# Expert tiles requested two at a time in a decoder step on one Trainium2 core

## What is computed

```python
q = (xt @ w_query)                         # 8 heads, 256 wide
s1, s2 = q[..., :128] @ k1.T, q[..., 128:] @ k2.T
v1, i1 = top_k(s1, 16); v2, i2 = top_k(s2, 16)
top, pos = top_k(v1[:, None] + v2[None, :], 16)    # 16 experts per head
g = softmax(top)
hid = u_tab[eidx] . xt                     # first layer: one dot product per expert
a = g * gelu(hid)
out = sum(a * v_tab[eidx])                 # second layer
```

## Time and profile before

| | |
|---|---|
| median of 3 runs | 1867.72 us (1864.65 to 1868.74) |
| profiled execution | 1864.95 us, span of the profile 1863.4 us |
| mean granted TensorE clock | 0.960 of full speed |
| TensorE busy | 1691.0 us, 91% of the span |
| VectorE busy | 1397.9 us, 75% |
| ScalarE busy | 776.9 us, 42% |
| GpSimd busy | 570.6 us, 31% |
| moved by DMA | 470.82 MB, mean 253 GB/s |
| requests of expert tiles | 128 of 512 KB, median 6.7 us from issue to landing |

### The profile page before, as it was taken

One profiled execution on the slowest core, in us unless ns is written; L12 is line 12 of the kernel. 1 busy time (PEld: TensorE's weight loads), 2 busy tenths in 40 slices (PEclk: granted clock), 3 DMA queues, 4 the chain that ended last, 5 costly groups with the idle time before them and its releaser, 6 DMA issues. The chain is left out here.

```text
span 1863.4 us, 30406 instructions
## 1 busy us (share of the span) xinstructions
PE 1691.0 (91%) x9914; PEld 1486.2 (80%) x9914; DVE 1397.9 (75%) x3179; ACT 776.9 (42%) x1195; POOL 570.6 (31%) x508
## 2 busy tenths in 40 slices
PE   5997898779799999779989999996899999999994
PEld 4997643449699999779989999996688888888883
DVE  3234267534389999968979888987898999999995
ACT  3222034221444433256657666663333333333333
POOL 0010280000354544433323333332433333333330
PEclk9998899899799999989999999998899999999997
DMA  3242361261343432379998998999999999999992
GB/s 112 97 174 94 121 214 46 83 232 43 116 143 111 138 115 82 124 259 350 345 376 304 366 354 332 380 338 361 363 386 387 384 384 384 384 384 389 385 385 81
DMA packets 195215, 470.82 MB, mean 253 GB/s; under 512 B 17922, under 2 KB 100482, under 8 KB 192558
## 3 DMA queue, kind: packets, MB, share of 16 engines
q1 hardware_dynamic: 124014, 240.30, 36.7%
q0 software_dynamic: 50944, 178.96, 26.0%
q10 hardware_dynamic: 20160, 50.34, 6.9%
HBM read 411.97 MB, written 61.32 MB: 254 GB/s over the span
## 5 line engine op out<-in xcount | busy, mean ns | idle before, releaser
L226 PE MATMUL hp<-mid_hi,uhi 128*128 128x384 f32 x1024 | 355.3, 347 | 12.0 <-issue 6.0
L227 PE MATMUL hp<-mid_lo,uhi 128*128 128x384 f32 x1024 | 345.7, 338 | 0.0
L228 PE MATMUL hp<-mid_hi,ulo 128*128 128x384 f32 x1024 | 344.4, 336 | 0.0
L226 PE MATMUL va<-vhi,ahi 128*128 128x512 f32 x768 | 299.6, 390 | 22.6 <-DVE alo L2010 22.6
L227 PE MATMUL va<-vlo,ahi 128*128 128x512 f32 x768 | 299.4, 390 | 0.0
L228 PE MATMUL va<-vhi,alo 128*128 128x512 f32 x768 | 299.2, 390 | 0.0
L2026 POOL DMA_INDIRECT gathered<-in_v_experts,idx_row x160 | 186.5, 1166 | 323.9 <-DVEq L1981 289.7
L1719 POOL DMA_INDIRECT gathered<-in_u_rows,idx_row x160 | 169.2, 1058 | 312.9 <-DVE hrow L1772 228.0
L226 PEld LDWEIGHTS hp<-mid_hi,uhi 128*128 128x128 f32 x1024 | 193.8, 189 | 17.3 <-DVE ulo L1785 8.6
L1316 ACT ACTIVATE uhi<-uw 128x1024 fp32r<-128x1024 f32 x128 | 135.7, 1060 | 151.9 <-PE hp L228 101.9
L1955 ACT ACTIVATE vhi<-vw 128x1024 fp32r<-128x1024 f32 x128 | 134.8, 1053 | 144.3 <-DMA vw<-in_v_experts 144.1
(11 more groups left out here) (328 smaller groups left out, 3306.2 us busy)
## 6 DMA issues: line engine op xcount, KB each, us to landing
uw<-in_u_experts SPq DMA_DIRECT2D x128, 512.0 KB, 6.7
vw<-in_v_experts SPq DMA_DIRECT2D x128, 512.0 KB, 10.6
hidden_values<-gelu_out ACTq DMA_DIRECT2D x128, 192.0 KB, 5.4
gate_matrix<-gst ACTq DMA_DIRECT2D x12, 2048.0 KB, 12.7
mid_hi<-hidden_values SPq DMA_DIRECT2D x32, 768.0 KB, 11.9
mid_lo<-gate_matrix SPq DMA_DIRECT2D x32, 768.0 KB, 16.6
pw<-in_w_qk SPq DMA_DIRECT2D x16, 512.0 KB, 3.5
qw<-in_w_query SPq DMA_DIRECT2D x16, 512.0 KB, 5.0
```

The costliest lines, as they stand in the source:

```text
L226: nc.tensor.matmul(out, a_hi, b_hi, start=first, stop=False)
L227: nc.tensor.matmul(out, a_hi, b_lo, start=False, stop=False)
L228: return nc.tensor.matmul(out, a_lo, b_hi, start=False, stop=last)
```

## The change

A request now covers two tiles, m and m+1, m even, and fills two neighbouring buffers, r and r+1, with 1 MB. It waits for the low half of tile m-3 (before: the request of m waited for that of m-4, the one of m+1 for that of m-3). Both tiles of a pair count on one semaphore, `u_load[r // 2]`, so ScalarE's high half of either tile waits until the whole pair has landed. The rows read stay 4 KB: the pattern is partition, tile, row.

```diff
-        u_load = [sem(f"u_load{i}") for i in range(UR)]
+        u_load = [sem(f"u_load{i}") for i in range(UR // 2)]
...
         def u_fetch(sp, m, r):
-            sp.wait_ge(u_lo, m + 3 - UR)
-            sp.dma_start(uw[:, r], A["u_experts"][m]).then_inc(u_load[r], 16)
+            sp.wait_ge(u_lo, m + 4 - UR)
+            sp.dma_start(uw[:, r:r + 2], A["u_experts"][bass.ds(m, 2)].rearrange("n p k c -> p n k c")).then_inc(u_load[r // 2], 16)
 
         def u_split_hi(act, m, i, r):
-            act.wait_ge(u_load[r], (m - r) * (16 // UR) + 16)
+            act.wait_ge(u_load[r // 2], (m - r) * (16 // UR) + 16)
...
-                for r in range(UR):
-                    sp.dma_start(uw[:, r], A["u_experts"][r]).then_inc(u_load[r], 16)
+                for r in range(0, UR, 2):
+                    sp.dma_start(uw[:, r:r + 2], A["u_experts"][r:r + 2].rearrange("n p k c -> p n k c")).then_inc(u_load[r // 2], 16)
...
-                    for r in range(RT):
+                    for r in range(0, RT, 2):
                         u_fetch(sp, RT * j + UR + r, r % UR)
-                for e in range(QX + UR):
+                for e in range(0, QX + UR, 2):
                     u_fetch(sp, RT * NH + e, e % UR)
...
-                    for i in range(GTI):
+                    for i in range(0, GTI, 2):
                         u_fetch(sp, G0 + GTI * j + i + UR, slot(half, i))
```

## The result

The changed kernel took 1881.45 us in the median of 20 executions (1871.25 to 1887.29), the kernel before 1866.89 in as many (1864.65 to 1873.72). The ratio is 1.0068, with an interval of 1.0053 to 1.0082: slower by 0.68%, or 12.7 us. (It is taken over all executions; the two medians by themselves are 14.6 us apart.) That lies above the range given, whose upper end was 1875. The profiled execution took 1885.38 us, and its span, 1883.8, is 20.4 longer than the one before.

A forecast was written before the change was run, and what follows sets the result against it. TensorE was taken to bound the gate stage, with the DMA engines close to full, and VectorE the retrieval stage's end. Four terms of 0 left the median at 1867.7 us, range 1862 to 1875.

The forecast's parts named there:

- Part 1: SyncE's requests: 128 become 64 and its issues of about 0.33 us halve, worth nothing by itself; cost 0.
- Parts 1 and 2: The second: at the first request, ScalarE's first high half waits for both tiles, about 1.3 us, covered by GpSimd; cost 0.
- Part 3: Even tiles, requested one tile later, still land in time; second 512 KB adds 1.7 us, under the 3.6 spare; cost 0.
- Rival C: Expert requests served by two of sixteen engines: 24 us per 1 MB, 500 us in all, near 2370; chance 0.01.
- rival A2: Gate stage: even tiles come too late for ScalarE's high half, 8.4 to 20.7 us slower, 1882; chance 0.05.
- Rival B: DMA queues in the gate stage: fewer requests relieve them, TensorE wins back 5.2 us, 1862.5; chance 0.13.
- part 4: Other transfers beside gate stores: help or hurt by at most 7.5 us, gain at most 5.2; taken as 0.
- Rival A: ScalarE's hidden-value stores behind gate stores held up to 1.5 us longer, five times, plus 1.1 for clock: 1876.3; chance 0.13.

The follow-up runs named there:

- the changed kernel's second profile: The changed kernel run again without further edits, against the kernel before on the same chip: 1873.63 us, ratio 1.0043; the profiled execution took 1865.83 us.
- joint landing alone: The kernel before, single requests at their old times, but one semaphore per pair so both high halves wait for both tiles: 1866.58 us, ratio 1.0000.
- one pair alone: The kernel before with one 1 MB request per turn, at i = 8, all others single at old times: 1883.30 us, ratio 1.0089.
- bunched singles: The kernel before with every even tile requested one tile later, still 128 requests of 512 KB; three runs: ratios 1.0009, 1.0018, 1.0008.
- the two runs made for it: Changed kernel with i = 8 pair as two singles at the pair's time: 1.0030; singles everywhere at the changed kernel's times, 1 MB only at i = 8: 1.0020.

## Why the prediction was wrong

**What held.** Part 1: SyncE's fewer issues gave nothing; an issue of 1 MB takes 0.37 us instead of 0.33. Parts 1 and 2 at zero: the retrieval stage has 330.7 us against 330.4, though ScalarE's first wait grew to 1.9 us. Part 3 held. The median landing in the gate stage was foretold at about 9 us and under 15.5 at most; the tile uw from 815 to 1320 us in the changed kernel's second profile:

```profile
DMA to landing us min/median/max: 5.3/9.7/15.4
```

The second half-megabyte adds 2.4 us to the median, where I took 1.7 and set the limit at 3.6; one high half was late, by 0.6 us. Part 3 also called the pair behind 577.58 us the tightest of the retrieval stage, with a lead of 15.7 us; the last four pairs of that stage (tiles 34 to 41) have less, 10.9, 9.8, 9.8 and 8.9 us from the odd request to the even tile's high half. With landings of 3.3 to 3.5 us there they were safe even so. That the joint landing costs nothing the run with joint landing alone shows by itself. Rival C fell (in that profile no landing is over 15.4 us, where it named over 20), and so did rival A2 as a cause; in the gate stage the changed kernel's three profiles have 0.6, 1.6 and 1.2 us of waits for tiles, and only with four buffers do whole pairs bring more (8.3 us in the whole execution). Rival B fell: the DMA engines gave nothing back. The fixed 2.0 us that it sets beside its 1.8 stand in the Trainium skill, "DMA: Bandwidth & Descriptors" (Anatomy of one DMA), as a fit on requests from GpSimd; the ones here are SyncE's.

**The step that failed is part 4**: "By the unchanged sum of bytes I take 0." It had two faults. The first is the place. I looked for gate stores "issued with an odd tile's request", found the worst hold of the kernel before there, and priced what would change at that store. There are two gate stores in a turn, and this is the second. Some of these the change holds longer and some less, by whether the pair goes out just ahead or just behind, and in sum they are held for 16.3 us against 17.9. The first gate store goes out 2.1 us behind an odd request and was harmless before, with holds of 1.55 to 2.80 us, and so I passed it over. There the change puts a whole tile in front. The second fault is the quantity. "At any moment the pairs have asked for no more than the single requests had" is true of what was requested so far, and beside the point: what a store has to share the engines with is what was requested and has not landed. At 2 us ahead of the gate store this doubled, from 512 KB to 1 MB.

**Rival A** (chance 0.13) had the right mechanism and sign: the stores held longer, TensorE behind them, a stretch at the lower clock behind that. Its place was wrong in the same way, and its price too low: five times 1.5 us and 1.1 for the clock, for 1876.3. Measured were six first gate stores with (28.1 - 13.4) / 6 = 2.4 us more each, 14.7 in all; TensorE's waits for low halves grew by 11.6. The 1.5 us was the bare time of 512 KB at 349 GB/s, and I let it stand as the bound of part 4 as well, five times; with one pair alone the first gate stores landed 2.2 us later on average, and 2.8 in the third turn. The clock's share was put at one more stretch at 0.68 over 3.5 us; measured were 13.7 us more at 0.50 in the gate stage. The Trainium skill, "DMA: Bandwidth & Descriptors" (Queues, rings and completion order), says that a DMA engine takes turns between the queues that have work, packet by packet. The later landings of the gate store and of the hidden-value store beside it (16.3 for 13.5, 9.6 for 7.1, in the third turn) agree with such sharing; no run here shows the order of packets.

**What is shown and what is open.** Shown: the loss arises at the pair of i = 8 (moved alone it gives 1.0093, left where it was 0.9988) and goes through ScalarE's two store buffers (with four, the holds are gone and both kernels are faster than before). Open: why the same request costs 0.9% when the others are at their old times, and 0.3 to 0.7% when all are bunched in pairs, and 0.1 to 0.2% when all are bunched singles. The second gate stores may be a part of it: in the seven profiles with all requests bunched the holds behind them add up to 10.1 to 16.3 us, in the three with the others at their old times to 17.5 to 21.9. But the kernel with joint landing alone, with old times, has 13.2 there against 17.9 before, so one profile each does not show it. Whether the 1 MB form adds something of its own at this place is left open by the two runs made for it (1.0030 and 1.0020); with all else as before it adds nothing that could be told (1.0089 against 1.0093, each to within 0.2 to 0.3%). Open also is why executions of the changed kernel differ by up to 20 us within one series (1863.48 to 1883.78), where those of the kernel before on the same chip differ by 13 (1860.69 to 1873.97). The order of pair and second gate store changes from one to the next (ahead in none, three and two of five turns in its second, third and first profile), and each time it does a hold changes by microseconds; what decides the order was not looked into.

## What to carry to other kernels

When a load is moved, list the big transfers of the other queues and ask of each what has been requested and not yet landed at that moment, before and after. The sum of bytes said nothing here, and the place that cost was one that had been harmless. Where a store goes out behind a large store in the same queue, see whether its buffers last for the time of the large one: two more of 192 KB gave 0.57% here and left at most 0.19% between the ways to issue the loads. Larger requests for loads that were hidden anyway brought nothing here.

## What the runs showed of the hardware

- Six requests of 128, each of 512 KB and issued some 6 us later, 2 us ahead of a store of 2 MB from another queue, cost 0.93% of the whole kernel; the bytes, the requests and the instructions are the same.
- A 2 MB store landed in 13.0 to 14.8 us when 1 MB was requested in another queue up to 0.9 us ahead of it (13 stores), and in 10.2 to 13.3 us when the same 1 MB was requested up to 0.3 us behind it (17 stores).
- Requests of 64 partitions by 2 tiles in place of 128 by 2 made the kernel 3% slower. Each took SyncE 0.60 us to issue, more than one of 1 MB over 128 partitions (0.37).
- A second 512 KB in the same request added 2.4 us to the median landing under load (9.7 for 7.3), with 1.5 us of bare data at 349 GB/s.
- Around an idle time of 3.66 us, from 1.1 us before its end, the granted clock was 0.50 for 6.8 us, of which TensorE worked 5.69.
